# In the loop of the seven products, the order of two splits is exchanged on ScalarE and on VectorE

## The chip, the cores and the metric

One core of a Trainium2 chip runs the whole program. The metric is the device time in microseconds (us) of one execution. TensorE does the matrix products, ScalarE, VectorE and GpSimd prepare their operands, and SyncE issues the loads.

## The reference

Two layers in float32, 512 tokens of width 1024. Each layer holds two feed-forward blocks (SwiGLU, inner width 2816), a mixer (gated linear attention in the first layer, a convolution module in the second), attention to a memory, and layer norms:

```python
def swiglu(x, w_gu, w_down):
    a, b = jnp.split(x @ w_gu, 2, axis=-1)
    return (jax.nn.silu(a) * b) @ w_down

for i in range(DEPTH):                      # DEPTH = 2
    x = layer_norm(ALPHA * x + 0.5 * swiglu(x, ffn1_w_gu[i], ffn1_w_down[i]), ln_g[i, 0], ln_b[i, 0])
    ...                                     # mixer and memory attention, with their norm
    x = layer_norm(ALPHA * x + 0.5 * swiglu(x, ffn2_w_gu[i], ffn2_w_down[i]), ln_g[i, 2], ln_b[i, 2])
```

So there are four feed-forward blocks. The change lies in their first product, `x @ w_gu`.

## The kernel before

**Precision.** Every float32 operand is cut into a high part in a reduced format and a low part, the remainder: `whi` and `wlo` for the weights in `raw`, `xhi` and `xlo` for the activations. Each product is three matmuls: high by high, high weight by low activation, low weight by high activation. ScalarE makes the high part by a copy that rounds (L661), VectorE the low part by a subtraction (L1112).

**Chunks and pairs.** The weights come in chunks of 1024 rows by 256 columns, 1 MB each, into `raw[:, s]` with s = 0 or 1. A pair is one chunk of gate columns (slot 0) and one of up columns (slot 1). A block has 11 pairs. The first two are multiplied plainly. Pairs 2 to 10 use a scheme with seven products in place of eight (Strassen and Winograd's): each chunk is seen as a 2 by 2 matrix of blocks, and besides its blocks the products need three sums of blocks.

**The loop of the seven products.** Nine pairs times four blocks make 36 pairs, or 72 chunks. TensorE works at one chunk for seven products of 12 matmuls of 256 columns, 84 in all. That stretch is called a half here. In each half the engines do this:

- SyncE loads the next weights into `raw[:, s]` as soon as the low part of the chunk that lay there is made (`lo_ready`).
- GpSimd makes the sums (L553, L555, L556, L560), each an addition of 512 elements in a partition. L553 and L555 write `s12[s]`, L556 changes a block of `raw` in place, and L560 writes `s4`, of which there is only one. So L560 waits until VectorE has read the `s4` of the chunk before (`ex_lo_ready`).
- ScalarE makes the high parts: of the chunk itself (L661, 2048 elements in a partition), and of the sums (`extra_hi`, L667 with 1024 and L668 with 512). Both wait until all four sums stand (`w_sum`). For a gate chunk it also applies silu (L692, four pieces).
- VectorE makes the low parts: of the chunk itself (`split_lo`, L1112) and of the sums (`extra_lo`, L1119 and L1122). Between them it combines partial results in PSUM in four steps (`combine`: L1167, L1169, L1172, L1175), each released by one of TensorE's products (`part_mm`), and once a pair it multiplies silu by up (L1204).

TensorE waits for these inside a half:

```python
pe.wait_ge(lo_ready, FFN_N[f] + 2 * i + g + 1)     # product 1: the chunk itself
pe.wait_ge(ex_lo_ready, 2 * q + 1)                 # product 2: the first two sums
pe.wait_ge(part_done, 4 * q + 1)                   # product 3: L1167
pe.wait_ge(part_done, 4 * q + 3)                   # product 5: L1172
pe.wait_ge(ex_lo_ready, 2 * q + 2)                 # product 6: the third sum
pe.wait_ge(part_done, 4 * q + 4)                   # product 7: L1175
```

(the lines between are left out). L1175 itself can start when product 5 has ended.

**Order.** There is no scheduler. Each engine runs its instructions in the order in which its own function writes them, and semaphores hold the engines together. In the second and third block VectorE and ScalarE also split a piece of the convolution's weights once a pair (L713, L1188, "early"). In the first block GpSimd also builds two tiles of diagonals in each of the pairs 2 to 7 (L585). Behind the last pair come the down projection's chunks, for which VectorE makes the low part of the hidden activations (`h_lo_parts`, L1140, 22 pieces of 512 elements).

Of the kernel before, what the change touches and what calls it, by code (L numbers as in the profile page):

```python
# [144 lines left out]
def summed(f, i, g):  # L145

    return SUMMED * f - 2 * PLAIN + 2 * i + g


def build(nc, a, out):  # L150
# [3 lines left out]
    with ExitStack() as ctx:  # L154
# [492 lines left out]
        def _(act):  # L647
            def split_hi(turn, s, kc=8, width=256, late=False, used=None):

                n = 2 * turn + s  # L650
                if isinstance(n, int) and n >= N_CHUNKS:
                    return
                if not isinstance(n, int) or n >= 2:
                    act.wait_ge(w_used, n - 1 if used is None else used)
                loads = turn + 1 if not isinstance(turn, int) or n < DIAG_N else turn + 3
                if late:
                    loads = turn + 3
                elif isinstance(n, int) and CONV_N <= n < DIAG_N:
                    loads += sum(c is not None for c in CONV_BLOCK[s:n - CONV_N + 1:2])
                act.wait_ge(raw_loaded[s], 16 * loads)  # L660
                nc.scalar.copy(whi[:, s, 0:kc, 0:width], raw[:, s, 0:kc, 0:width]).then_inc(hi_ready, 1)  # L661

            def extra_hi(f, i, s):

                q = summed(f, i, s)
                act.wait_ge(w_sum, 4 * q + 4)
                nc.scalar.copy(ex_hi[s][:, 0:2], s12[s][:, :, :, :]).then_inc(ex_hi_ready, 1)  # L667
                nc.scalar.copy(ex_hi[s][:, 2], s4).then_inc(ex_hi_ready, 1)  # L668

            def next_hi(f, i, s):  # L670

                last = isinstance(i, int) and i == FK // 2 - 1
                if not isinstance(i, int) or PLAIN <= i + 1 < FK // 2:
                    act.wait_ge(w_sum, 4 * summed(f, i + 1, s) + 4)
                split_hi(FFN_N[f] // 2 + i + 1, s, DOWN_K[s] if last else 8, late=f == 3)
# [5 lines left out]
            def ffn_pair(f, i):  # L681

                by_sums = not isinstance(i, int) or i >= PLAIN
                sums_next = not isinstance(i, int) or PLAIN <= i + 1 < FK // 2
                act.wait_ge(w_used, FFN_N[f] + 2 * i + 1)
                next_hi(f, i, 0)
                if not isinstance(i, int) or f + i > 0:
                    act.wait_ge(mul_done, gated_by(f, i))
                if by_sums:
                    for n, b in enumerate((0, 3, 2, 1)):  # L690
                        tok = slice(n % 2 * HALF, n % 2 * HALF + HALF)
                        nc.scalar.activation(act_out[n // 2][:, tok], bank[b][:, tok], ACT.Silu).then_inc(silu_done, 1)  # L692
                else:
                    for t in range(2):
                        nc.scalar.activation(act_out[t], bank[t][:, :], ACT.Silu).then_inc(silu_done, 1)
                if sums_next:
                    extra_hi(f, i + 1, 0)
                if isinstance(i, int) and i == FK // 2 - 1:
                    act.wait_ge(mul_done, gated_by(f, i))
                    h_hi_parts(f, range(KEPT))  # L700
                act.wait_ge(w_used, FFN_N[f] + 2 * i + 2)
                next_hi(f, i, 1)
                if sums_next:
                    extra_hi(f, i + 1, 1)
                if isinstance(i, int) and i == 0:
                    if f == 0:
                        act.wait_ge(kv_stored, 64)
                    for j, (to, _, _) in enumerate(T_SUM):
                        act.wait_ge(t_sum, 4 * f + j + 1)
                        nc.scalar.copy(t_hi[:, j], to).then_inc(t_hi_ready, 1)  # L710
                if f in (1, 2) and (not isinstance(i, int) or 0 < i <= EARLY):
                    act.wait_ge(early_loaded, 16 * (EARLY * (f - 1) + i))
                    nc.scalar.copy(early_hi[:, :, :], early_raw[:, :, :]).then_inc(early_hi_done, 1)  # L713
# [392 lines left out]
        def _(dve):  # L1106
            def split_lo(n, s, kc=8, width=256):

                dve.wait_ge(hi_ready, n + 1)
                if not isinstance(n, int) or n:  # L1110
                    dve.wait_ge(lo_ready, n)
                nc.vector.tensor_tensor(wlo[:, s, 0:kc, 0:width], raw[:, s, 0:kc, 0:width],  # L1112
                                        whi[:, s, 0:kc, 0:width].bitcast(F32), ALU.subtract).then_inc(lo_ready, 1)

            def extra_lo(f, i, s):

                q = summed(f, i, s)
                dve.wait_ge(ex_hi_ready, 2 * q + 1)
                nc.vector.tensor_tensor(ex_lo[s][:, 0:2], s12[s][:, :, :, :], ex_hi[s][:, 0:2].bitcast(F32),  # L1119
                                        ALU.subtract).then_inc(ex_lo_ready, 1)  # L1120
                dve.wait_ge(ex_hi_ready, 2 * q + 2)
                nc.vector.tensor_tensor(ex_lo[s][:, 2], s4, ex_hi[s][:, 2].bitcast(F32), ALU.subtract).then_inc(ex_lo_ready, 1)  # L1122
# [14 lines left out]
            def h_lo_parts(f, ks):  # L1137
                for k in ks:
                    dve.wait_ge(h_hi_done, FK * f + k + 1)
                    nc.vector.tensor_tensor(h_lo[:, k, :], hid[:, k, :], h_hi[:, k, :].bitcast(F32), ALU.subtract).then_inc(h_done, 1)  # L1140
# [19 lines left out]
            def combine(f, i, g, step):  # L1160

                q, b = summed(f, i, g), 4 * g
                r1, r5 = bank[b][:, 0:HALF], bank[b + 1][:, HALF:SEQ]
                r6, r3 = bank[b + 2][:, 0:HALF], bank[b + 3][:, HALF:SEQ]
                dve.wait_ge(part_mm, 4 * q + step + 1)
                if step == 0:
                    nc.vector.tensor_scalar(r6, r1, -1.0, None, ALU.mult).then_inc(part_done, 1)  # L1167
                elif step == 1:
                    nc.vector.tensor_copy(p5_copy[:, :], r5).then_inc(part_done, 1)  # L1169
                elif step == 2:  # L1170
                    dve.wait_ge(part_done, 4 * q + 2)
                    nc.vector.scalar_tensor_tensor(out=r3, in0=r6, scalar=-1.0, in1=p5_copy[:, :], op0=ALU.mult,  # L1172
                                                   op1=ALU.subtract).then_inc(part_done, 1)
                else:
                    nc.vector.tensor_tensor(r5, r6, p5_copy[:, :], ALU.add).then_inc(part_done, 1)  # L1175

            def summed_pair(f, i):

                n, last = FFN_N[f] + 2 * i, isinstance(i, int)
                for step in range(3):  # L1180
                    combine(f, i, 0, step)
                split_lo(n + 1, 1)
                combine(f, i, 0, 3)
                extra_lo(f, i, 1)
                if f in (1, 2):
                    dve.wait_ge(early_hi_done, EARLY * (f - 1) - 1 + i)
                    dve.wait_ge(early_stored, 16 * (EARLY * (f - 1) - 1 + i))
                    nc.vector.tensor_tensor(early_lo[:, :, :], early_raw[:, :, :], early_hi[:, :, :].bitcast(F32),  # L1188
                                            ALU.subtract).then_inc(early_done, 1)
                for step in range(3):  # L1190
                    combine(f, i, 1, step)
                split_lo(n + 2, 0, DOWN_K[0] if last else 8)
                if last:
                    h_lo_parts(f, range(2))
                combine(f, i, 1, 3)
                if last:
                    h_lo_parts(f, range(2, KEPT))
                else:
                    extra_lo(f, i + 1, 0)
                dve.wait_ge(w_used, n + 2)  # L1200
                for m, b in enumerate((4, 7, 6, 5)):
                    tok = slice(m % 2 * HALF, m % 2 * HALF + HALF)
                    dve.wait_ge(silu_done, gated_by(f, i) + m + 1)
                    nc.vector.tensor_tensor(hid[:, bass.ds(2 * i + m // 2, 1), tok],  # L1204
                                            act_out[m // 2][:, tok].rearrange("p (a s) -> p a s", a=1),
                                            bank[b][:, tok].rearrange("p (a s) -> p a s", a=1), ALU.mult).then_inc(mul_done, 1)
# [1238 lines left out]
```

## Time and profile before

| | |
|---|---|
| median of three runs | 2054.97 us (2053.71 to 2055.51) |
| profiled execution, its own time | 2053.88 us |
| its span, first to last instruction | 2052.2 us |
| TensorE (PE) busy | 2022.4 us, 99% of the span |
| VectorE (DVE) busy | 1349.7 us, 66% |
| ScalarE (ACT) busy | 813.0 us, 40% |
| GpSimd (POOL) busy | 737.5 us, 36% |
| granted TensorE clock, mean | 0.996 of full speed |
| chain of work that ended last | 83% on PE, 6% on DVE, 5% on POOL |

A busy PE is one that has a matmul under way. Shares over the whole span mix stages with different limits, so the loops are read by themselves. PEld is the loading of weights into TensorE, which runs beside the matmuls.

### The profile page before, as it was taken

To read this page: it belongs to the slowest core of one execution; us is meant where nothing else is said; L and a number is where in the kernel's file an instruction comes from. 1 tells how busy PE (TensorE), PEld (TensorE's weight loads), DVE (VectorE), ACT (ScalarE), POOL (GpSimd) and SP (SyncE) were. 2 spreads that over 40 slices of the span, in tenths; PEclk is the share of its full clock that TensorE was granted. 3 is DMA by queue.
4 is the path that set the end of the run, shared out by engine and by line. 5 is a ranking of instruction groups with operands and counts; after the bars stand their busy time and mean duration, and the time that the engine had idled before them with its cause. 6 is when DMAs were issued, how large, how long until landed. Compare 5 with 4: busy or idle time off the path is not lost.

```text
span 2052.2 us, 34350 instructions
## 1 busy us (share of the span) xinstructions
PE 2022.4 (99%) x13509; PEld 1856.7 (90%) x13509; DVE 1349.7 (66%) x1842; ACT 813.0 (40%) x1163; POOL 737.5 (36%) x443
## 2 busy tenths in 40 slices
PE   9999999999999999999999999999999899999998
PEld 9899998988988989999898999889887699999887
DVE  4477774554435767777466788646899786766645
ACT  5433451253423344444234444423453434434422
POOL 1488720043312247770014777001100324776000
PEclk9999999999999999999999999999999999999999
DMA  7544322332211234443232545223544322332232
GB/s 250 185 144 157 129 87 92 110 105 77 68 32 62 93 114 151 156 162 101 94 106 93 164 144 170 99 95 113 175 133 160 103 71 92 104 102 92 88 102 89
DMA packets 229497, 239.13 MB, mean 117 GB/s; under 512 B 5983, under 2 KB 222173, under 8 KB 227612
## 3 DMA queue, kind: packets, MB, share of 16 engines
q1 hardware_dynamic: 228764, 235.68, 35.3%
q10 hardware_dynamic: 640, 2.16, 0.3%
q8 instruction: 64, 1.05, 0.2%
q14 instruction: 29, 0.24, 0.0%
HBM read 215.80 MB, written 22.02 MB: 116 GB/s over the span
## 4 chain that ended last, share of the span: by engine, by line
PE 83%; DVE 6%; POOL 5%; issue 3%; ACT 2%; DMA 0%; SPq 0%; DVEq 0%; POOLq 0%; ACTq 0%
PE bank L1756 11%; PE bank L1757 11%; PE bank L1758 11%; PE bank L1885 10%; PE bank L1887 10%; PE bank L1886 10%; PE bank L1767 3%; PE bank L1768 3%; PE bank L1769 3%; DVE u L1665 2%; POOL xlo L531 1%; ACT whi L661 1%; POOL s L553 1%; POOL diag_tmp L585 1%; PE bank L1839 1%
## 5 line engine op out<-in xcount | busy, mean ns | idle before, releaser
L661 ACT CAST whi<-raw 128x2048 fp32r<-128x2048 f32 (+2 forms) x192 | 326.3, 1701 | 881.3 <-POOL scratch L560 441.6
L1112 DVE TENSOR_TENSOR wlo<-raw,whi 128x2048 fp32r<-128x2048 f32 (+2 forms) x166 | 365.1, 2200 | 244.9 <-ACT whi L661 244.5
L537 POOL TENSOR_TENSOR tiny<-tiny 128x2 f32<-128x2 f32 (+1 forms) x13 | 9.4, 726 | 754.5 <-DVE tiny L1383 754.5
L556 POOL TENSOR_TENSOR raw<-raw 128x512 f32<-128x512 f32 x72 | 216.9, 3012 | 0.0
L1756 PE MATMUL bank<-h_hi,whi 128*128 128x512 f32 x528 | 207.1, 392 | 0.0
L1757 PE MATMUL bank<-h_lo,whi 128*128 128x512 f32 x528 | 205.5, 389 | 0.0
L1758 PE MATMUL bank<-h_hi,wlo 128*128 128x512 f32 x528 | 205.5, 389 | 0.0
L1885 PE MATMUL bank<-t_hi,whi 128*128 128x256 f32 x576 | 163.6, 284 | 5.2 <-DVE bank L1175 5.2
L1756 PE MATMUL bank<-xhi,whi 128*128 128x512 f32 x400 | 160.7, 402 | 3.3 <-DVE wlo L1112 3.3
L1887 PE MATMUL bank<-xhi,wlo 128*128 128x256 f32 x576 | 163.0, 283 | 0.0
L1885 PE MATMUL bank<-t_hi,ex_hi 128*128 128x256 f32 x576 | 163.0, 283 | 0.0
L1886 PE MATMUL bank<-t_lo,ex_hi 128*128 128x256 f32 x576 | 163.0, 283 | 0.0
L1887 PE MATMUL bank<-t_hi,ex_lo 128*128 128x256 f32 x576 | 163.0, 283 | 0.0
L1886 PE MATMUL bank<-xlo,whi 128*128 128x256 f32 x576 | 163.0, 283 | 0.0
L1887 PE MATMUL bank<-t_hi,wlo 128*128 128x256 f32 x576 | 163.0, 283 | 0.0
L1885 PE MATMUL bank<-xhi,whi 128*128 128x256 f32 x576 | 163.0, 283 | 0.0
L1886 PE MATMUL bank<-t_lo,whi 128*128 128x256 f32 x576 | 163.0, 283 | 0.0
L1758 PE MATMUL bank<-xhi,wlo 128*128 128x512 f32 x400 | 156.9, 392 | 0.0
L1757 PE MATMUL bank<-xlo,whi 128*128 128x512 f32 x400 | 156.8, 392 | 0.0
L560 POOL TENSOR_TENSOR scratch<-raw,s 128x512 f32<-128x512 f32 x72 | 106.7, 1483 | 121.0 <-DVE ex_lo L1122 121.0
L553 POOL TENSOR_TENSOR s<-raw 128x512 f32<-128x512 f32 x72 | 105.8, 1469 | 97.2 <-DVE t_lo L1135 56.8
L514 POOL TENSOR_TENSOR wlo<-raw,whi 128x2048 fp32r<-128x2048 f32 (+1 forms) x17 | 74.0, 4355 | 168.6 <-ACT whi L661 168.6
(351 smaller groups left out, 5868.5 us busy)
## 6 DMA issues: line engine op xcount, KB each, us to landing
raw<-in_ffn_w_gu_dram SPq DMA_DIRECT2D x88, 1024.0 KB, 4.9
raw<-in_ffn_w_down_dram SPq DMA_DIRECT2D x32, 896.0 KB, 5.1
raw<-in_ffn_w_down_dram SPq DMA_DIRECT2D x32, 512.0 KB, 3.4
raw<-in_gla_w_in_dram SPq DMA_DIRECT2D x14, 1024.0 KB, 5.1
early_raw<-in_conv_w_in_dram SPq DMA_DIRECT2D x18, 512.0 KB, 4.2
lo_scratch<-early_lo SPq DMA_DIRECT2D x18, 512.0 KB, 3.2
diag_scratch<-diag_tmp SPq DMA_DIRECT2D x8, 1024.0 KB, 8.7
raw<-in_conv_w_in_dram SPq DMA_DIRECT2D x16, 512.0 KB, 5.4
```

The source lines that it names most:

```text
L514: nc.gpsimd.tensor_tensor(wlo[:, s, 0:kc, 0:width], raw[:, s, 0:kc, 0:width], whi[:, s, 0:kc, 0:width].bitcast(F32), ALU.subtract).then_in ...
L553: nc.gpsimd.tensor_tensor(s12[s][:, 0], a21, a22, ALU.add).then_inc(w_sum, 1)
L556: nc.gpsimd.tensor_tensor(a21, a21, a11, ALU.add).then_inc(w_sum, 1)
L560: nc.gpsimd.tensor_tensor(s4, a12, s12[s][:, 1], ALU.add).then_inc(w_sum, 1)
L661: nc.scalar.copy(whi[:, s, 0:kc, 0:width], raw[:, s, 0:kc, 0:width]).then_inc(hi_ready, 1)
L1112: nc.vector.tensor_tensor(wlo[:, s, 0:kc, 0:width], raw[:, s, 0:kc, 0:width], whi[:, s, 0:kc, 0:width].bitcast(F32), ALU.subtract).then_in ...
L1756: nc.tensor.matmul(to, w_hi[:, k, w], hi, start=start, stop=False)
L1757: nc.tensor.matmul(to, w_hi[:, k, w], lo, start=False, stop=False)
L1758: return nc.tensor.matmul(to, w_lo[:, k, w], hi, start=False, stop=stop)
L1885: nc.tensor.matmul(to, w_hi[:, k], hi[:, k], start=(start and k == 0), stop=False, skip_group_check=True)
L1886: nc.tensor.matmul(to, w_hi[:, k], lo[:, k], start=False, stop=False, skip_group_check=True)
L1887: last = nc.tensor.matmul(to, w_lo[:, k], hi[:, k], start=False, stop=(k == 3), skip_group_check=True)
```

## The change

On both engines the parts of the sums now come ahead of the parts of the chunk itself.

```diff
@@ ffn_pair (ScalarE)
                 act.wait_ge(w_used, FFN_N[f] + 2 * i + 1)
+                if sums_next:
+                    extra_hi(f, i + 1, 0)
                 next_hi(f, i, 0)
...
                         nc.scalar.activation(act_out[t], bank[t][:, :], ACT.Silu).then_inc(silu_done, 1)
-                if sums_next:
-                    extra_hi(f, i + 1, 0)
...
                 act.wait_ge(w_used, FFN_N[f] + 2 * i + 2)
-                next_hi(f, i, 1)
                 if sums_next:
                     extra_hi(f, i + 1, 1)
+                next_hi(f, i, 1)
@@ summed_pair (VectorE)
                 for step in range(3):
                     combine(f, i, 0, step)
+                extra_lo(f, i, 1)
+                combine(f, i, 0, 3)
                 split_lo(n + 1, 1)
-                combine(f, i, 0, 3)
-                extra_lo(f, i, 1)
...
                 for step in range(3):
                     combine(f, i, 1, step)
+                if last:
+                    h_lo_parts(f, range(2))
+                else:
+                    extra_lo(f, i + 1, 0)
+                combine(f, i, 1, 3)
                 split_lo(n + 2, 0, DOWN_K[0] if last else 8)
                 if last:
-                    h_lo_parts(f, range(2))
-                combine(f, i, 1, 3)
-                if last:
                     h_lo_parts(f, range(2, KEPT))
-                else:
-                    extra_lo(f, i + 1, 0)
```

TensorE, GpSimd and SyncE keep their instructions in their order.

VectorE, body of the first block's loop, the half with the up chunk, before (register rows belong to the waits; `wlo` is the chunk's low part, `ex_lo` the sums', `bank` PSUM):

```order
L1172 SCALAR_TENSOR_TENSOR bank<-bank,p_copy 128x256
L1109 REGISTER_ALU
L1112 TENSOR_TENSOR wlo<-raw,whi 128x2048
L1165 REGISTER_ALU
L1175 TENSOR_TENSOR bank<-bank,p_copy 128x256
L1118 ISA
L1119 TENSOR_TENSOR ex_lo<-s_0,ex_hi 128x1024
L1121 REGISTER_ALU
L1122 TENSOR_TENSOR ex_lo<-scratch,ex_hi 128x512
L1203 ISA
```

The same place now:

```order
L1172 SCALAR_TENSOR_TENSOR bank<-bank,p_copy 128x256
L1118 ISA
L1119 TENSOR_TENSOR ex_lo<-s_0,ex_hi 128x1024
L1121 REGISTER_ALU
L1122 TENSOR_TENSOR ex_lo<-scratch,ex_hi 128x512
L1165 REGISTER_ALU
L1175 TENSOR_TENSOR bank<-bank,p_copy 128x256
L1109 REGISTER_ALU
L1112 TENSOR_TENSOR wlo<-raw,whi 128x2048
L1203 ISA
```

The split of 2048 elements has moved from ahead of the fourth combining step to behind it, and the sums' two splits from behind it to ahead of it. The half with the gate chunk moves in the same way.

ScalarE, the same loop, the second half of its body, before (`whi` is the chunk's high part, `ex_hi` the sums'):

```order
L674 ISA
L661 CAST whi<-raw 128x2048
L667 CAST ex_hi<-s_1 128x1024
L668 CAST ex_hi<-scratch 128x512
```

The same place now:

```order
L666 ISA
L667 CAST ex_hi<-s_1 128x1024
L668 CAST ex_hi<-scratch 128x512
L661 CAST whi<-raw 128x2048
```

The chunk's high part now stands behind the sums' two, and in the first half of the body, which also holds the silu pieces, it does as well.

VectorE, the last pair of a block and the start of the down projection, before:

```order
L1172 SCALAR_TENSOR_TENSOR bank<-bank,p_copy 128x256
L1112 TENSOR_TENSOR wlo<-raw,whi 128x1024
L1140 TENSOR_TENSOR h_lo<-hid,h_hi 128x512 x2
L1175 TENSOR_TENSOR bank<-bank,p_copy 128x256
L1140 TENSOR_TENSOR h_lo<-hid,h_hi 128x512 x4
L1204 TENSOR_TENSOR hid<-scratch,bank 128x256 x4
```

The same place now:

```order
L1172 SCALAR_TENSOR_TENSOR bank<-bank,p_copy 128x256
L1140 TENSOR_TENSOR h_lo<-hid,h_hi 128x512 x2
L1175 TENSOR_TENSOR bank<-bank,p_copy 128x256
L1112 TENSOR_TENSOR wlo<-raw,whi 128x1024
L1140 TENSOR_TENSOR h_lo<-hid,h_hi 128x512 x4
L1204 TENSOR_TENSOR hid<-scratch,bank 128x256 x4
```

Here a split of half the size moves behind the fourth combining step.

## Rows read from the trace of the kernel before

**Rows 1.** Windows, three stretches: us, busy us of PE, PEld, DVE, ACT, POOL, clock.
```profile
90.00:300.00 210.00, 204.82 (x1610) 199.84 (x1609) 155.54 (x182) 82.23 (x109) 155.17 (x84) 1.00 0.41 133
752.00:949.00 197.00, 197.00 (x1582) 194.35 (x1581) 145.39 (x178) 84.51 (x109) 132.07 (x72) 1.00 0.44 145
1590.00:1620.00 30.00, 24.27 (x99) 17.83 (x98) 26.47 (x37) 9.62 (x10) 9.42 (x3) 0.91 0.27 88
```

**Rows 2.** Waits, whole span: us in total, times, longest.
```profile
PE bank L1885 <- DVE bank L1175: 5.2, 6, 1.2
```

**Rows 3.** Timeline of VectorE, second loop: start us, us, instruction, [idle before].
```profile
842.56 2.75 DVE L1112 TENSOR_TENSOR wlo<-raw,whi 128x2048 fp32r<-128x2048 f32 x1
...
862.38 0.43 DVE L1172 SCALAR_TENSOR_TENSOR bank<-bank,p_copy 128x256 f32<-128x256 f32 x1 [1.01 <-PE bank L1887]
862.72 2.73 DVE L1112 TENSOR_TENSOR wlo<-raw,whi 128x2048 fp32r<-128x2048 f32 x1
...
872.46 0.43 DVE L1172 SCALAR_TENSOR_TENSOR bank<-bank,p_copy 128x256 f32<-128x256 f32 x1 [1.01 <-PE bank L1887]
```

**Rows 4.** Timeline of GpSimd, the same stretch.
```profile
850.59 1.29 POOL L553 TENSOR_TENSOR s<-raw 128x512 f32<-128x512 f32 x1 [1.00 <-DMA raw<-in_ffn_w_gu_dram]
...
862.00 1.29 POOL L555 TENSOR_TENSOR s<-s,raw 128x512 f32<-128x512 f32 x1
863.25 3.35 POOL L556 TENSOR_TENSOR raw<-raw 128x512 f32<-128x512 f32 x1
...
870.55 1.30 POOL L553 TENSOR_TENSOR s<-raw 128x512 f32<-128x512 f32 x1 [0.83 <-DMA raw<-in_ffn_w_gu_dram]
```

**Rows 5.** Timeline of TensorE: the first matmul of a half.
```profile
867.94 0.28 PE L1885 MATMUL bank<-xhi,whi 128*128 128x256 f32 x1
```

**Rows 6.** Timeline of ScalarE, the half that begins at 867.94.
```profile
869.75 1.91 ACT L661 CAST whi<-raw 128x2048 fp32r<-128x2048 f32 x1 [4.56 <-POOL scratch L560]
...
872.52 0.61 ACT L668 CAST ex_hi<-scratch 128x512 fp32r<-128x512 f32 x1
```

**Rows 7.** Timeline of VectorE, first loop: a fourth combining step.
```profile
166.63 0.42 DVE L1175 TENSOR_TENSOR bank<-bank,p_copy 128x256 f32<-128x256 f32 x1
```

**Rows 8.** Timeline of TensorE around it: a wait for that step.
```profile
166.02 0.28 PE L1887 MATMUL bank<-xhi,ex_lo 128*128 128x256 f32 x1
167.11 0.38 PE L1885 MATMUL bank<-t_hi,whi 128*128 128x256 f32 x1 [0.81 <-DVE bank L1175]
167.33 0.28 PE L1886 MATMUL bank<-t_lo,whi 128*128 128x256 f32 x1
```

**Rows 9.** Timeline of GpSimd, first loop.
```profile
174.21 3.34 POOL L553 TENSOR_TENSOR s<-raw 128x512 f32<-128x512 f32 x1
177.64 2.15 POOL L555 TENSOR_TENSOR s<-s,raw 128x512 f32<-128x512 f32 x1
```

**Rows 10.** Timeline of VectorE, the same microseconds.
```profile
176.66 1.98 DVE L1119 TENSOR_TENSOR ex_lo<-s,ex_hi 128x1024 fp32r<-128x1024 f32 x1
178.56 1.77 DVE L1122 TENSOR_TENSOR ex_lo<-scratch,ex_hi 128x512 fp32r<-128x512 f32 x1
```

**Rows 11.** Timeline of VectorE, second loop's last pair, and the down projection's start.
```profile
933.28 2.28 DVE L1112 TENSOR_TENSOR wlo<-raw,whi 128x2048 fp32r<-128x2048 f32 x1
935.82 0.43 DVE L1175 TENSOR_TENSOR bank<-bank,p_copy 128x256 f32<-128x256 f32 x1 [0.26 <-PE bank L1887]
936.16 1.22 DVE L1119 TENSOR_TENSOR ex_lo<-s,ex_hi 128x1024 fp32r<-128x1024 f32 x1
...
957.99 4.91 DVE L1140 TENSOR_TENSOR h_lo<-hid,h_hi 128x512 fp32r<-128x512 f32 x8
```

**Rows 12.** GpSimd's last sums (L560), second loop: ns min/median/max, first and last start.
```profile
L560 POOL TENSOR_TENSOR scratch<-raw,s x18: 1290/1299/2150, 757.3 to 928.5; 128x512 f32<-128x512 f32 x18
```

**Rows 13.** Timeline of TensorE: the down projection's third chunk begins.
```profile
959.48 0.39 PE L1756 MATMUL bank<-h_hi,whi 128*128 128x512 f32 x1
```

**Rows 14.** All splits of L1112 in 800 to 920 us: ns min/median/max.
```profile
L1112 DVE TENSOR_TENSOR wlo<-raw,whi x12: 2324/2608/2766, 802.2 to 913.1; 128x2048 fp32r<-128x2048 f32 x12
```

## The prediction

> **What bounds the kernel now.** The windows come first: TensorE is busy through the whole of the second loop, 197.00 of 197.00 us, at full clock [rows 1]. In the first loop, where GpSimd also builds diagonals, it is busy 204.82 of 210 us, and the list of waits gives the reason: six times TensorE waits for the fourth combining step L1175, 5.2 us together [rows 2]. So the loops run at TensorE's own rate. That rate shows in VectorE's timeline, where the third combining step L1172, released by TensorE each time, starts at 862.38 and 872.46 [rows 3]: a half lasts 10.08 us, 84 matmuls 0.12 us apart, seven products of 1.44 us. Nothing in the loops can become much faster than this; there are only the first loop's stalls to win. The question is thus how much slack the moved work had.
>
> Now put S = 0 at the first matmul of a half, 867.94 [rows 5]. L1172 starts at 872.46, S + 4.52. The fourth step, where it waits for nothing but TensorE, starts at 935.82 [rows 11]. That is in the half that begins six halves later, at 867.94 + 6 x 10.08 = 928.42, so at S + 7.40. Both of these times are set by TensorE's products, whatever VectorE does between. Before, VectorE starts the 2048 split L1112 0.34 us after L1172 started (862.38, 862.72) [rows 3], at about S + 4.86. Over all twelve of 800 to 920 us the split takes 2.32 to 2.77 us [rows 14]. It is done by S + 7.6, and TensorE needs its result at the next half's first product, S + 10.08. There were 2.5 us of slack.
>
> **The change, step by step.** No instruction is added or removed. On ScalarE the high part of the chunk moves behind two copies. They end at 872.52 + 0.61 = 873.13, and the chunk's high part started at 869.75 and took 1.91 [rows 6], so the copies cost 1.47 us of delay. I cost this at nothing. The high part would end near S + 5.2, and the split that reads it will start only at S + 8. If that cover were gone (were the sums late by 3 us) each microsecond more would be paid in full. Silu comes later by the same 1.5 us, and has until the end of the next half.
>
> On VectorE the split is now behind L1175, and it is the last thing before the half's end. L1175 has the next instruction 0.34 us behind it (935.82, 936.16) [rows 11]. So the split starts at S + 7.74 at best. Alone, it takes 2.28 us, as at 933.28 [rows 11], when GpSimd has nothing more to do (the last of its sums begins at 928.5 [rows 12]). It would end at S + 10.02, and the hand-off to TensorE takes 0.06 (L1175 ends at 166.63 + 0.42 = 167.05, the matmul starts at 167.11) [rows 7, 8]. That is S + 10.08, just in time: the whole slack is used up before anything else is counted. Two things come on top.
>
> First, a matmul that was waited for has its second matmul 0.22 us behind it (167.11, 167.33) [rows 8] and not 0.12. A stalled half thus pays another 0.10 us, and all its later times move by as much.
>
> Second, GpSimd and VectorE exclude each other in these operations. L556 starts at 863.25, but ends 1.15 us after the end of VectorE's split (865.45), at 866.60 [rows 3, 4]. The split itself began at 862.72, while L555 ran until 863.29, and ended 2.16 us after that. In the first loop one sees a whole row of it [rows 9, 10]: L553 ends at 177.55, L1119 1.09 us later at 178.64, L555 1.15 us later at 179.79, L1122 0.54 us later at 180.33. Each waits for the other's instruction and then needs nearly its own length; they take turns.
>
> When does GpSimd run? It waits for the load, and the load for the split's end. L553 starts 5.28 us after the split's end at 845.31 (850.59), and 5.10 us after that at 865.45 (870.55) [rows 3, 4]. The next half begins 0.06 after the split's end, so L553 arrives at S + 5.04 to 5.22 of the new half. It will always arrive there, because both hang on the same split. The half, with its 0.10 us, is then:
>
> - L1172 starts at 4.62, L1119 at 4.96. Alone it takes 1.22 [rows 11] and ends at 6.18.
> - L553 arrives at 5.04 to 5.22, waits, and ends at 6.18 + 1.15 = 7.33.
> - L1122 waits for it and ends at 7.33 + 0.54 = 7.87.
> - L555 waits for that and ends at 7.87 + 1.15 = 9.02.
> - L1175 reads PSUM. It starts at 7.79, ahead of product 7, which wants it by 8.74. The split starts at 8.13, waits for L555 until 9.02 and ends at 9.02 + 2.16 = 11.18.
> - TensorE starts the next half at 11.24.
>
> So a half grows by 1.16 us. L556 and L560 follow in the next half's first 2 us, ScalarE copies after them, and the sums' high parts stand near S + 4, ahead of 4.96; the early split L1188 lies in the time of L1167. Behind the moved split on VectorE are L1204, L1188 and the steps L1167 and L1169. They are wanted by product 3 at the earliest, 2.9 us into the half, and lose nothing.
>
> Of the 18 halves of a block, 16 hold a 2048 split with GpSimd at work: 16 x 1.16 = 18.6 us. In the first half of the last pair GpSimd is silent and it costs 0.10. The second half has a small split, with room. Behind the last pair VectorE is late by that small split, some 1.1 us (a 1024 operation is 1.22 [rows 11], and its successor starts 0.09 before its end). The first L1140 of the second eight starts at 957.99 and takes about 0.61 [rows 11], so it ends at 958.6, and the down projection's third chunk wants it at 959.48 [rows 13]. It will end at 959.7: a stall of 0.3 us, with the 0.10. A block loses 19.0 us, four lose 76. The first loop's six stalls of some 0.97 us each (1.09 between two matmuls in place of 0.12 [rows 8]) I leave as they are: L1175 is freed of the split, but product 1 now waits behind the same busy GpSimd. Bounds for this term: 0 and -6.
>
> The profiled execution took 2053.88 us, with a span of 2052.2, and stands 1.1 us under the median of the runs. The forecast is 2053.9 + 76 = **2130 us**.
>
> The Trainium skill, page "SBUF — State Buffer", section "SBUF: two separate sides", calls this port between VectorE and GpSimd "an exclusive lock": it is held for a whole instruction, and a VectorE operation with two SBUF inputs takes it as well. By this rule the trace agrees where L1119 stretches from 1.22 to 1.98 us [rows 10, 11], but a waiting instruction ends earlier there than its full length after the release. By the page's words alone each would need its full length, and the time would be that of the first rival below.
>
> **The rivals.**
>
> *Full length after each release.* With 1.30 for GpSimd's additions, 0.61 for L1122 (as one L1140, of the same size [rows 11]) and 2.28 for the split, the chain gives 6.18 + 1.30 + 0.61 + 1.30 + 2.28 + 0.06 = 11.73, 1.65 us a half: 106 us, 2160. Against it speaks that L1119, L555 and L1122 ended 1.09, 1.15 and 0.54 us after the release [rows 9, 10].
>
> *The engines meet only partly,* and the split takes what it took before, 2.32 to 2.77, mostly 2.6 (turns lost at L1119). A half is then 0.10 + 7.74 + 2.6 + 0.06 = 10.50 (10.22 to 10.67): 0.42 x 64 = 27 us, 2081 (2063 to 2093). For it speaks that L553 arrives only 0.1 to 0.3 us behind L1119's start; against it, that a long split needs GpSimd at work at S + 8, where it is in any order.
>
> *GpSimd first.* If L553 gets ahead of L1119, it ends at 6.2, L1119 at 7.3, L555 at 8.45, L1122 at 9.0. L1175 is then late for product 7, L556 ends at 10.15 and the split at 12.3: 2.3 us a half, 147 us, 2201. It needs a load only 0.1 to 0.3 us quicker, so it cannot be excluded; in single halves it may well occur.
>
> *The clock.* The stretch behind the convolution was busy 24.27 of 30 us and had a granted clock of 0.91 [rows 1]. A loop with a tenth of idle time at that level would cost about another 70 us, 2200. The first loop, busy at 98%, had 1.00.
>
> *Not slower.* If GpSimd and VectorE do not meet at the split at all, it takes 2.28: 0.10 a half, 7 us, less the first loop's 6: 2055, no change. If on top the first split catches every half's start, there are no stalls at all, and the six waits for L1175 go: 2048. The point that decides is a split of 2.28 us or less; the shortest of twelve was 2.32.
>
> **How the numbers follow.** The chain as worked out: 0.62, with its own range 2118 to 2142 (the length of a half by 0.15 us either way). Partly: 0.13. Full length: 0.04. GpSimd first: 0.10. The clock or another added wait: 0.03. No change: 0.05. Faster: 0.03. The range goes from the partly case to the full-length case, 2078 to 2166. It leaves out the last four and a little of the second. A difference of under 0.2%, 4 us, could not be told from none. Slower by more than that has 0.92, the same 0.05, faster 0.03.
>
> **What the changed profile would show.** TensorE's list of waits should have a new line, its first matmul of a half (L1885) on L1112, some 64 times, about 1.05 us each. L1172 should return every 11.24 us. L1112 should take 3.0 us in place of 2.6, L1119 1.2 in place of 1.98, L1122 near 1.8, and L553 near 2.1 us. ScalarE's L661 should wait less for L560, since `s4` comes free earlier, and that should bring nothing. The six waits for L1175 may stay or go. The prediction is wrong if L1172 still returns at 10.08 us, or if L553 is found ahead of L1119.

## The result

The changed kernel takes 2122.42 us (median of four runs, 2121.31 to 2123.49) against 2054.34 us before. The ratio is 1.0333, with a 95% interval of 1.0321 to 1.0345: 3.3% slower, 68 us. Its profiled execution took 2123.49 us with a span of 2121.8; 69.6 us over that of before.

The windows of the first and the second loop, busy us of each engine (the stretches lie inside the loops):

```profile
core 0: us, PE busy (x) PEld busy (x) DVE busy (x) ACT busy (x) POOL busy (x), PEclk, DMA share, GB/s
90.00:300.00 210.00, 195.94 (x1533) 189.54 (x1533) 140.01 (x161) 74.86 (x98) 157.21 (x84) 1.00 0.38 124
780.00:960.00 180.00, 165.84 (x1351) 162.69 (x1350) 145.27 (x153) 70.32 (x88) 132.34 (x64) 1.00 0.41 138
```

The granted clock is 1.00 in both stretches. TensorE, busy without a gap in the second loop before [rows 1], is now idle in 8% of it. The list of waits, whole span (us in total, times, longest), names what TensorE waits for. Of its waits inside the loops there are two kinds:

```profile
PE bank L1885 <- DVE wlo L1112: 55.5, 56, 1.5
...
PE bank L1885 <- DVE bank L1175: 1.9, 4, 0.5
```

The upper line is new: 56 times TensorE waits at the first matmul of a half for the 2048 split L1112. L1175, waited for six times before [rows 2], is waited for four times, and briefly. One half of the second loop shows how it comes about. VectorE's timeline:

```profile
866.22 3.04 DVE L1112 TENSOR_TENSOR wlo<-raw,whi 128x2048 fp32r<-128x2048 f32 x1
...
873.93 0.43 DVE L1172 SCALAR_TENSOR_TENSOR bank<-bank,p_copy 128x256 f32<-128x256 f32 x1 [1.02 <-PE bank L1887]
874.28 1.22 DVE L1119 TENSOR_TENSOR ex_lo<-s,ex_hi 128x1024 fp32r<-128x1024 f32 x1
875.41 1.79 DVE L1122 TENSOR_TENSOR ex_lo<-scratch,ex_hi 128x512 fp32r<-128x512 f32 x1
877.12 0.42 DVE L1175 TENSOR_TENSOR bank<-bank,p_copy 128x256 f32<-128x256 f32 x1
877.46 3.04 DVE L1112 TENSOR_TENSOR wlo<-raw,whi 128x2048 fp32r<-128x2048 f32 x1
...
885.17 0.43 DVE L1172 SCALAR_TENSOR_TENSOR bank<-bank,p_copy 128x256 f32<-128x256 f32 x1 [1.01 <-PE bank L1887]
```

and GpSimd's beside it:

```profile
874.50 2.15 POOL L553 TENSOR_TENSOR s<-raw 128x512 f32<-128x512 f32 x1 [2.83 <-DMA raw<-in_ffn_w_gu_dram]
876.73 1.62 POOL L555 TENSOR_TENSOR s<-s,raw 128x512 f32<-128x512 f32 x1
878.31 3.33 POOL L556 TENSOR_TENSOR raw<-raw 128x512 f32<-128x512 f32 x1
```

The half lasts 885.17 - 873.93 = 11.24 us, where it was 10.08 [rows 3]. The five operations take turns. L553 arrives 0.22 us behind L1119 and waits for it, L1122 waits for L553 (1.79 us), L555 for L1122, and the split, which starts 3.53 us behind L1172 where it was 0.34 before [rows 3], waits for L555 (until 878.35) and ends 2.15 us after that, at 880.50. L556 then waits for the split. On TensorE the hand-off at the start of this half looks like this:

```profile
869.32 0.39 PE L1885 MATMUL bank<-xhi,whi 128*128 128x256 f32 x1 [0.90 <-DVE wlo L1112]
869.54 0.28 PE L1886 MATMUL bank<-xlo,whi 128*128 128x256 f32 x1
```

The split before it ended at 866.22 + 3.04 = 869.26; the half's first matmul starts 0.06 us later, the second 0.22 us after the first, as in [rows 8].

The length of each loop is read from the fourth combining step, 18 in a loop (first and last start at the end of the times). Before, the first and the third loop (the second and the fourth took 171.3 us each):

```profile
L1175 DVE TENSOR_TENSOR bank<-bank,p_copy x18: 419/420/433, 112.3 to 290.4; 128x256 f32<-128x256 f32 x18
...
L1175 DVE TENSOR_TENSOR bank<-bank,p_copy x18: 419/420/433, 1128.8 to 1300.0; 128x256 f32<-128x256 f32 x18
```

and of the changed kernel, all four:

```profile
L1175 DVE TENSOR_TENSOR bank<-bank,p_copy x18: 419/420/433, 113.2 to 302.9; 128x256 f32<-128x256 f32 x18
...
L1175 DVE TENSOR_TENSOR bank<-bank,p_copy x18: 419/420/433, 788.0 to 976.8; 128x256 f32<-128x256 f32 x18
...
L1175 DVE TENSOR_TENSOR bank<-bank,p_copy x18: 419/420/433, 1160.8 to 1349.5; 128x256 f32<-128x256 f32 x18
...
L1175 DVE TENSOR_TENSOR bank<-bank,p_copy x18: 420/420/433, 1790.7 to 1980.6; 128x256 f32<-128x256 f32 x18
```

The first loop has grown from 178.1 to 189.7 us, the third from 171.2 to 188.7. In the first half of a loop L1175 now comes 3.6 us after its L1172 and came 2.9 us after it before, while in the last half it waits for TensorE alone in both. So 0.6 to 0.8 us are to be added: the loops lost 12.4, 18.2, 18.1 and 19.4 us, 68.1 in all, of the span's 69.6.

The first loop does not repeat one half as the others do. Up to 242 us its halves take 11.7 to 12.2 us and 10.2 us in turn. In the six short ones L553 arrives 6.7 to 6.8 us behind the end of the split, where it is 5.0 in the loop's last pairs, and L1119 and L1122 are then out of the way. These are the six halves in which SyncE has issued a store of the diagonals right behind the load. In one of them, the row of the store's issue (SPq is SyncE's queue) and GpSimd's row of the late addition:

```profile
161.29 0.58 SPq L349 DMA_DIRECT2D diag_scratch<-diag_tmp  x1
...
167.54 1.30 POOL L553 TENSOR_TENSOR s<-raw 128x512 f32<-128x512 f32 x1 [3.04 <-DMA raw<-in_ffn_w_gu_dram]
```

Behind the last store GpSimd is sometimes first. Three halves then last 12.3 to 12.4 us, and in each of them L553 starts 0.02 to 0.05 us ahead of L1119. In one of them, GpSimd's row and VectorE's:

```profile
254.29 1.29 POOL L553 TENSOR_TENSOR s<-raw 128x512 f32<-128x512 f32 x1 [3.85 <-DMA raw<-in_ffn_w_gu_dram]
254.31 2.36 DVE L1119 TENSOR_TENSOR ex_lo<-s,ex_hi 128x1024 fp32r<-128x1024 f32 x1
```

### The profile page after: what moved, and what is told of

Read it like the earlier page. It is cut to its first block, busy times and chain, and to the rows that moved or that the text cites. A ratio compares the mean times of both kernels' runs of the same rounds, so it can differ in the third digit from the quotient of the medians.

```text
span 2121.8 us, 34350 instructions
## 1 busy us (share of the span) xinstructions
PE 2039.9 (96%) x13509; PEld 1860.0 (88%) x13509; DVE 1394.6 (66%) x1842; ACT 812.2 (38%) x1163; POOL 778.2 (37%) x443
## 4 chain that ended last, share of the span: by engine, by line
PE 66%; DVE 16%; POOL 7%; issue 5%; DMA 4%; ACT 2%; DVEq 0%; SPq 0%; POOLq 0%; ACTq 0%
PE bank L1756 11%; PE bank L1758 11%; PE bank L1757 11%; DVE wlo L1112 7%; PE bank L1885 5%; PE bank L1887 4%; PE bank L1886 4%; DMA raw<-in_ffn_w_gu_dram 3%; PE bank L1767 3%; PE bank L1768 3%; PE bank L1769 3%; DVE ex_lo L1122 3%; POOL raw L556 2%; DVE u L1665 2%; DVE ex_lo L1119 2%
## 5 line engine op out<-in xcount | busy, mean ns | idle before, releaser
L1112 DVE TENSOR_TENSOR wlo<-raw,whi 128x2048 fp32r<-128x2048 f32 (+2 forms) x166 | 380.4, 2292 | 241.0 <-ACT whi L661 240.7
L667 ACT CAST ex_hi<-s 128x1024 fp32r<-128x1024 f32 x72 | 75.5, 1049 | 511.1 <-POOL scratch L560 493.8
L1885 PE MATMUL bank<-xhi,whi 128*128 128x256 f32 x576 | 169.8, 295 | 55.5 <-DVE wlo L1112 55.5
L553 POOL TENSOR_TENSOR s<-raw 128x512 f32<-128x512 f32 x72 | 128.2, 1780 | 228.6 <-DMA raw<-in_ffn_w_gu_dram 163.1
L556 POOL TENSOR_TENSOR raw<-raw 128x512 f32<-128x512 f32 x72 | 189.2, 2628 | 0.0
L1885 PEld LDWEIGHTS bank<-xhi,whi 128*128 128x128 f32 x576 | 109.8, 191 | 67.6 <-DVE wlo L1112 66.8
```

What stands on the lines that cost most here:

```text
L553: nc.gpsimd.tensor_tensor(s12[s][:, 0], a21, a22, ALU.add).then_inc(w_sum, 1)
L556: nc.gpsimd.tensor_tensor(a21, a21, a11, ALU.add).then_inc(w_sum, 1)
L1885: nc.tensor.matmul(to, w_hi[:, k], hi[:, k], start=(start and k == 0), stop=False, skip_group_check=True)
```

## The experiments

Each ratio is against runs of the kernel before on the same chip.

**Which engine's part.** `e1_scalar_only` changes ScalarE alone, `e2_vector_only` VectorE alone.

```diff
 # e1: the kernel before, with
+                    extra_hi(f, i + 1, 0)        # and (f, i + 1, 1); the calls further down go
                 next_hi(f, i, 0)                 # and (f, i, 1)
 # e2: the changed kernel, with ffn_pair as it was before
```

> Only ScalarE's part of the change: the sums' high parts ahead of the chunk's high part; VectorE keeps its old order. Theory A (the time is lost because the 2048 split stands behind the fourth combining step on VectorE, and there takes turns with GpSimd): most of the loss goes. The split has to wait for a high part that ends some 1.5 us later, near S + 5.3 of a half in place of 4.9, and so ends at about 8.0 to 8.6; product 7 wants the fourth step at 8.7, so some halves lose 0 to 0.5 us. I expect 2080 us, between 2054 and 2090, and where TensorE waits, it waits for L1175, not for L1112. Theory B (the later high part on ScalarE is the cause): about 2122 us, with waits for L1112.

> Only VectorE's part of the change; ScalarE keeps its old order, so the sums' high parts come last. Theory A: the split is behind the fourth step as in the changed kernel, and L1119 can now also wait for its high part, which is made behind the chunk's own (1.9 us) and, in every second half, behind the silu pieces (1.1 us). At least 2122 us; more likely 2150 to 2210, with product 2 or product 7 waited for as well. Theory B: about 2054 us.

e1: 2081.22 us, ratio 1.0134 (1.0117 to 1.0151). e2: 2185.35 us, 1.0634 (1.0617 to 1.0652). TensorE's waits in e1, then in e2:

```profile
PE bank L1885 <- DVE bank L1175: 25.4, 28, 1.9
PE bank L1885 <- DVE bank L1167: 0.7, 1, 0.7
```

```profile
PE bank L1885 <- DVE wlo L1112: 66.8, 58, 1.5
PE bank L1885 <- DVE bank L1175: 39.6, 33, 2.7
```

In e1 no half waits for the split; 28 wait for L1175, which stands behind it. VectorE's timeline shows the place in e1:

```profile
856.78 0.43 DVE L1172 SCALAR_TENSOR_TENSOR bank<-bank,p_copy 128x256 f32<-128x256 f32 x1 [1.02 <-PE bank L1887]
858.86 2.72 DVE L1112 TENSOR_TENSOR wlo<-raw,whi 128x2048 fp32r<-128x2048 f32 x1 [1.65 <-ACT whi L661]
```

The split could start 0.34 us behind L1172, at 857.12, but waits for its high part until 858.86. So ScalarE's part costs 27 us by itself, in every second half, by making the split late ahead of L1175. VectorE's part alone costs 131 us, more than both together: with the split moved, ScalarE's exchange is needed, since the sums' low parts now come first. The loss comes from VectorE's part, and ScalarE's takes back about half of it. Theory B is out.

Some of e2's loss is clock and not order. In its second loop the granted clock was lower, where the changed kernel had 1.00:

```profile
780.00:960.00 180.00, 159.05 (x1172) 152.44 (x1170) 124.53 (x130) 61.95 (x76) 104.55 (x60) 0.95 0.36 120
```

It was 0.66 between 830 and 840 us, behind 10 us in which TensorE was busy for 8.03. In e2's first loop the clock was 1.00, and there the fourth combining steps show what the order costs alone:

```profile
L1175 DVE TENSOR_TENSOR bank<-bank,p_copy x18: 417/420/433, 112.6 to 319.2; 128x256 f32<-128x256 f32 x18
```

These are 206.6 us, against 189.7 in the changed kernel and 178.1 before.

**GpSimd's turns.** `e3_small_sums_new` and `e4_small_sums_old` leave out most of the sums: GpSimd adds only 8 of 128 columns, and the sums' parts are made from `xhi`. The first is built on the changed kernel, the second on the kernel before.

```diff
-                nc.gpsimd.tensor_tensor(s12[s][:, 0], a21, a22, ALU.add)
+                nc.gpsimd.tensor_tensor(s12[s][:, 0, :, few], a21[:, :, few], a22[:, :, few], ALU.add)
 ...                                             # few = slice(0, 8); the other three likewise
-                nc.scalar.copy(ex_hi[s][:, 0:2], s12[s][:, :, :, :])
+                nc.scalar.copy(ex_hi[s][:, 0:2], xhi[:, 0:2, :] ...)   # same size
```

> The changed kernel, but GpSimd's four additions work on 8 of 128 columns (32 elements in a partition in place of 512), and the sums' high and low parts are made from parts of the activations of the same size; so the products with the sums are others. ScalarE, VectorE and TensorE keep all instructions, sizes and waits. Theory A: without GpSimd to take turns with, the split takes 2.28 us and a half 10.18 us in place of 11.24; the time falls to 2054 + 68 x 0.10 - 6 = 2055 us, at most 2065. Theory C (VectorE's longer chain alone is the cause, or the loads, and GpSimd only happens to be there): 2115 to 2125 us.

> The same cut of GpSimd's additions in the kernel before, as the control. Theory A: nothing in loops two to four, which have no stall (10.08 us a half before and after); the first loop's six waits for L1175 (5.2 us and 0.10 each, about 6 us) go if GpSimd's turns made the split late there, which gives 2048 us. Theory C: no change, 2054 us.

e3: 2056.15 us, ratio 1.0011 (1.0001 to 1.0020). e4: 2047.34 us, 0.9968 (0.9957 to 0.9979). VectorE's timeline in e3 (its lines are one higher: L1173 is the third combining step, L1113 the split):

```profile
847.57 0.43 DVE L1173 SCALAR_TENSOR_TENSOR bank<-bank,p_copy 128x256 f32<-128x256 f32 x1 [1.01 <-PE bank L1888]
...
849.04 0.74 DVE L1123 TENSOR_TENSOR ex_lo<-xhi,ex_hi 128x512 fp32r<-128x512 f32 x1
...
850.79 2.28 DVE L1113 TENSOR_TENSOR wlo<-raw,whi 128x2048 fp32r<-128x2048 f32 x1
...
857.74 0.43 DVE L1173 SCALAR_TENSOR_TENSOR bank<-bank,p_copy 128x256 f32<-128x256 f32 x1 [1.01 <-PE bank L1888]
```

The order is the new one, the split still stands behind L1176, but it takes 2.28 us in place of 3.04, L1123 takes 0.74 in place of 1.79, and the half lasts 10.17 us. This fits the 10.18 of the expectation for a split that meets nobody. e4, the control, is 7 us faster than the kernel before. With GpSimd's additions short the new order thus costs 2056.15 - 2047.34 = 8.8 us in place of 68.

The 7 us are the stalls that the kernel before has in its first loop. The split of the half in [rows 7, 8] shows how they came about:

```profile
163.67 3.04 DVE L1112 TENSOR_TENSOR wlo<-raw,whi 128x2048 fp32r<-128x2048 f32 x1 [1.21 <-ACT whi L661]
```

It started late, behind a high part that had itself waited for GpSimd's last sum, and then it was long, behind L555. e4 takes away both, so it does not tell how much of the 7 us is lateness and how much is turns.

**The order of arrival.** `e5_short_load_new` is the changed kernel with shorter loads, 224 of 256 columns, so that GpSimd comes ahead of VectorE. The last columns of each chunk keep old data, so its products are others.

```diff
-                        load(n0 + 2 * i, 0, cols(w_gu, i * 256))
+                        load(n0 + 2 * i, 0, cols(w_gu, i * 256, 224))   # and the up chunk
```

> The changed kernel, but each gate and up load brings 224 of 256 columns, so the last columns of each chunk are old data; nothing else changes. The load lands some 0.5 us sooner, and so GpSimd's L553 should arrive at about S + 4.6, ahead of VectorE's L1119 (S + 4.96), not behind it. Theory A with turns in order of arrival: the order of turns changes (L553, L1119, L555, L1122, L556, split), L1175 comes late for product 7 and the split ends near S + 12.3. A half grows from 11.24 to about 12.4 us, and the time to 2170 to 2205 us: a smaller load makes the kernel slower. Rival (VectorE has priority, or the order of arrival doesn't matter): 2110 to 2125 us.

Measured: 2157.00 us, ratio 1.0496 (1.0479 to 1.0514), and 1.6% over the changed kernel: with less to load it is slower. TensorE's waits, then VectorE's and GpSimd's timelines of one half:

```profile
PE bank L1885 <- DVE wlo L1112: 69.4, 59, 1.3
PE bank L1885 <- DVE bank L1175: 12.8, 37, 0.5
```

```profile
856.97 0.43 DVE L1172 SCALAR_TENSOR_TENSOR bank<-bank,p_copy 128x256 f32<-128x256 f32 x1 [1.01 <-PE bank L1887]
857.31 2.17 DVE L1119 TENSOR_TENSOR ex_lo<-s,ex_hi 128x1024 fp32r<-128x1024 f32 x1
859.41 1.78 DVE L1122 TENSOR_TENSOR ex_lo<-scratch,ex_hi 128x512 fp32r<-128x512 f32 x1
...
869.14 0.43 DVE L1172 SCALAR_TENSOR_TENSOR bank<-bank,p_copy 128x256 f32<-128x256 f32 x1 [1.01 <-PE bank L1887]
```

```profile
857.11 1.29 POOL L553 TENSOR_TENSOR s<-raw 128x512 f32<-128x512 f32 x1 [2.40 <-DMA raw<-in_ffn_w_gu_dram]
858.48 2.15 POOL L555 TENSOR_TENSOR s<-s,raw 128x512 f32<-128x512 f32 x1
860.60 1.72 POOL L556 TENSOR_TENSOR raw<-raw 128x512 f32<-128x512 f32 x1
```

L553 runs unhindered (1.29 us), and L1119 takes 2.17. The split waits for L556 and the half lasts 12.17 us. But not every half is like that: of the eleven between 809 and 941 us, three lasted 11.23, as in the changed kernel. In these three L553 came level with L1119 or behind it and was the one that waited (2.25 to 2.37 us); in the eight long ones (12.1 to 12.3 us) it came first. So the order of arrival decides the length of a half, and the expected 2170 to 2205 was missed because the order is not the same in each half. The first loop hardly changed (191.2 us between its first and last L1172, against 190.5).

**The split's place alone.** `e6_split_behind_step` is the kernel before with one exchange.

```diff
-                split_lo(n + 1, 1)
                 combine(f, i, 0, 3)
+                split_lo(n + 1, 1)               # and the same with the gate chunk
```

> The kernel before with one exchange on VectorE alone: the fourth combining step L1175 ahead of the 2048 split, the sums' low parts behind the split as before; ScalarE unchanged. It parts the place of the split from the order of the sums. If the place is enough to cost the time: the split starts at S + 7.8, waits for none or for one of GpSimd's additions (2.28 to 3.3 us), and ends at S + 10.1 to 11.1, so 0.1 to 1.1 us a half and 2060 to 2125 us; I expect 2110. If it needs the sums' low parts ahead of it (a load of turns in S + 5 to 8): close to 2054 us.

Measured: 2138.49 us, ratio 1.0412 (1.0395 to 1.0430), above my 2125. TensorE's waits, and VectorE's timeline:

```profile
PE bank L1885 <- DVE wlo L1112: 32.7, 56, 1.0
PE bank L1885 <- DVE bank L1167: 10.8, 32, 0.6
PE bank L1885 <- DVE ex_lo L1119: 6.9, 13, 0.5
```

```profile
851.21 0.43 DVE L1175 TENSOR_TENSOR bank<-bank,p_copy 128x256 f32<-128x256 f32 x1 [2.45 <-PE bank L1887]
851.55 2.94 DVE L1112 TENSOR_TENSOR wlo<-raw,whi 128x2048 fp32r<-128x2048 f32 x1
854.42 1.21 DVE L1119 TENSOR_TENSOR ex_lo<-s,ex_hi 128x1024 fp32r<-128x1024 f32 x1
```

The place alone is enough. The 32.7 us of waits for the split are fewer than in the changed kernel (2.94 us, not 3.04), but now the sums' low parts run beyond the half's end, and products 2 and 3 wait as well (L1119, L1167), which I had not counted. Whether the sums should come first then depends on ScalarE: with its exchange they should (the changed kernel, 2122.42 us, against 2138.49 here), with its old order they should not (e2, 2185.35 us).

**A lighter GpSimd in the first loop.** e4 pointed to a version that could beat the kernel before and still compute the same. `e7_diagonals_scalar` keeps the old order and gives six diagonal tiles of the first loop to ScalarE; `e8_diagonals_scalar_new` does the same in the changed kernel.

```diff
-                if i < 2 * len(TAPS_K):
-                    diagonal(i)                  # GpSimd
+                for t in range(2):               # ScalarE, once a pair
+                    for j in range(kc):
+                        last = nc.scalar.activation(diag_tmp[:, j, t * P:(t + 1) * P], ident[:, :], ACT.Copy,
+                                                    scale=values[:, tap:tap + 1])
```

> The kernel before, with six of the eight diagonal tiles of the first loop built by ScalarE (14 or 16 scaled copies of 128 columns each) and not by GpSimd; the order of the splits is the old one. Theory A: GpSimd's 3.3 to 3.8 us a pair for the diagonals were what made ScalarE's high part and then the split late in the first loop. Without them its six stalls go: 5.2 us of waits and 0.10 each, 2048.5 us. ScalarE has over 8 us of idle time in each pair for the copies. Rival (the first loop's stalls come from something else, as the stores of the diagonals, or ScalarE becomes late itself): 2054 us or more.

> The same with the changed order of the splits. In the changed kernel the first loop lost less than the other three (some 12 us against 17 to 19), and every second half there took 10.17 us in place of 11.24. Theory A: there the diagonals shift GpSimd's additions so that the split meets none of them in one half of two. Without the diagonals the first loop behaves like the others: all halves near 11.24 us, 16 x 1.16 = 18.6 us over a loop without stalls, and the time is 2048 + 4 x 18 = 2120 us, no better than the changed kernel, although GpSimd has less to do. Rival (GpSimd's load in all decides): some 6 to 12 us below the changed kernel, 2110 to 2116 us.

e7: 2048.64 us, ratio 0.9971 (0.9960 to 0.9982), 0.3% faster than the kernel before; only e4, which leaves out most of the sums, is faster. e8: 2121.52 us, 1.0319 (1.0303 to 1.0336), the same as the changed kernel. The first loop's window in e7, to be read against the first line of [rows 1], and the fourth combining step (here L1193) in e8's first loop:

```profile
90.00:300.00 210.00, 209.62 (x1636) 204.56 (x1635) 153.06 (x189) 114.07 (x206) 123.03 (x72) 1.00 0.40 135
```

```profile
L1193 DVE TENSOR_TENSOR bank<-bank,p_copy x18: 418/420/433, 112.6 to 301.7; 128x256 f32<-128x256 f32 x18
```

In e7 TensorE's idle time in the stretch falls from 5.2 to 0.4 us. In e8 the first loop is about as long as in the changed kernel (189.1 us against 189.7). The time was as forecast, but not the picture, so the agreement is luck: the halves still alternate, near 10.2 and 11.2 to 12.3 us. So GpSimd's work on the diagonals is not the reason for the short halves. Their stores are still there, and the same six halves are short, with L553 again 6.8 to 6.9 us behind the split's end. That points to the stores, which delay the load that L553 waits for; no run leaves them out, so it is not shown.

## Why the prediction was right

**The slack of the moved split** held to 0.01 us in the half shown. The split was to start at S + 8.13 and the half to last 11.24 us. With S = 869.32 it starts at S + 8.14 and the half lasts 11.24; e3 shows that without GpSimd it would be 10.17.

**The turns between VectorE and GpSimd** were the cause: with the long additions gone (e3 against e4) 8.8 of the 68 us are left, and another order of arrival (e5) changes the size and makes a smaller load cost more. That L553 "will always arrive there" was wrong. In the second loop it lies 0.1 to 1.0 us behind L1119 in the halves of 11.24, and it can lie anywhere there, because it waits for L1119 and L1122 waits for it. In the first loop it comes too late for these turns in six halves, and first in three. L553 ahead of L1119 was named as a sign of being wrong, and it shows there in 3 of 17 halves. These three are the rival "GpSimd first", at 12.3 to 12.4 us a half, where 12.4 was worked out; e5 shows it in most of its halves.

**The rivals.** The "full length" reading is out, since the split ended 2.15 us after L555 and not 2.28. The partly case (2.6 us for the split) did not come: nearly all splits inside the loops take about 3.04 us, or about 2.3 in the short halves. The clock stayed at 1.00 in the changed kernel's loops, with TensorE 92% busy in the second; in e2, where it was 88% busy, it was 0.95, so this rival was not far off.

**ScalarE's part costed at nothing** holds inside the change, where the high part has until S + 8. It is no general figure: with the old order on VectorE the cover is gone, and e1 shows 27 us.

**The term that was mis-sized** is the first loop's: I let the six stalls of before stand and added 19 us, with bounds of 0 and -6. The loop lost 12.4 us, so the bound of -6 was nearly the right value. Before, it ran 178.1 - 171.2 = 6.9 us longer than a loop without stalls. These stalls are gone, and the loop is now 19 us longer than one without stalls, like the others. That it comes so near to them is luck: six short halves make up for ones of 11.8 and 12.3 us, and none of this was in the chain. The other three loops lost 18.2, 18.1 and 19.4 us where I had 18.7. Of the 7.9 us between 76 and 68.1 the first loop makes 6.3. The stall of 0.3 us at each down projection isn't seen among the waits; it was a term of 1 us. The range of the main case, given as 0.15 us a half either way, comes to 10 us on each side of 2130 and not to 12.

## What to carry to other kernels

Before an instruction is moved behind one that another engine releases, work out when it can start at the latest and when its result is wanted, in the period of the loop. Here 2.5 us of slack were used up by the move, and what was left over was decided by a neighbour that the diff doesn't name.

Where two engines take turns, the cost of an order is read from who arrives first. If a load hangs on the end of the moved instruction, its arrival moves along, and the meeting recurs turn after turn. Other transfers may still shift it, as the stores seem to do in the first loop here.

Stalls of the old kernel should not be carried over into a slower loop without a look: here the new waits took their place.

## What the runs showed of the hardware

- A load of an eighth fewer bytes made the kernel 1.6% slower (e5), by letting GpSimd's addition in ahead of VectorE's subtraction.
- GpSimd waits for VectorE as VectorE waits for it: in the changed kernel L553 took 2.15 us and L556 3.33 us, where L553 alone takes 1.30 [rows 4]. The Trainium skill, page "SBUF — State Buffer", section "SBUF: two separate sides", calls the port an exclusive lock held for the whole instruction. The rows here agree, with one refinement: a waiting instruction ends about 0.13 us sooner after the release than its length alone (2.15 us for a split that takes 2.28, 1.15 for an addition that takes 1.30).
- 88 scaled copies of 128 columns on ScalarE were free beside the loop (e7): ScalarE's busy time in the 210 us rose from 82.23 [rows 1] to 114.07 us, and TensorE's idle time did not rise with it.
- A lead of 0.02 us decided 1.1 us of a half in the changed kernel's first loop: 12.35 us with L553 at 254.29 and L1119 at 254.31, 11.23 in the next half with L1119 at 266.66 and L553 at 266.67.
